# S5's scan by doubling replaced by a turning frame, and the mixer's steps in a new order

## The chip, the cores and the metric

The program runs on one core of a Trainium2 chip. The metric is the device time of one launch in microseconds. The engines are named as the profile names them: PE (TensorE matmul), PEld (its weight load), DVE (VectorE), ACT (ScalarE), POOL (GpSimd), SP (the queue that starts the weight DMAs).

## The reference, cut to what matters

Two transformer blocks run on 256 tokens of width 1024, all in float32. The first block's mixer has four branches (RWKV-7 `a`, spatial gating `b`, short convolution `c`, S5 `d`), whose outputs are gated and summed:

```python
h = rms_norm(x, norm_mix_g) * (1.0 + sc1) + sh1
p = h @ w_in
y_d = s5_mixer(p[..., OFF_D:OFF_G], ...)
gates = sigmoid(p[..., OFF_G:]).reshape(bsz, seq, 4, D_MODEL)
merged = gates[0] * y_a + gates[1] * y_b + gates[2] * y_c + gates[3] * y_d
x = x + gt1 * (merged @ w_o)
```

S5 has 16 groups of 64 complex states, 1024 states in all. Each state follows x[t] = ab * x[t-1] + bu[t] over the 256 tokens:

```python
mag = exp(lam_re * dt)
ab_re, ab_im = mag * cos(lam_im * dt), mag * sin(lam_im * dt)
q = (ab - 1) / lam                      # written out in real and imaginary parts
bb = q[..., None] * b                   # the gain q sits on the input matrix
bu = einsum('gnc,bsgc->bsgn', bb, u)
x = associative_scan(_complex_affine_combine, (ab, bu), axis=1)
y = einsum(c_re, x_re) - einsum(c_im, x_im) + d * u
y_d = glu(gelu(y) @ glu_w)
```

What follows (a feed-forward part, and the second block with its attention and the gathered experts) is not touched.

## The kernel before

The kernel writes one instruction list for each engine by hand. A list runs in order, and engines meet by semaphores. Weights stream through a ring of three slots of 2 MB each, in the order of `STREAM`. The SP queue issues tile n when the tile before it in the same slot has been used.

The mixer's order is the same on all engines. `mixer_order` (L45) walks over 18 projection chunks p0 to p18 (p11 belongs to p10), then over 32 gate parts (8 weight tiles, 2 row tiles, 2 halves), the `ada` sums, the merges, and between them it calls steps. `SCHEDULE` (L30) has one string for each place: `"ad"` behind a chunk means one step of branch a, then one step of branch d. Every engine has a generator for each branch that it serves, and a step is what stands between two `yield`s. So one letter in `SCHEDULE` puts a step at the same place of all lists.

S5's states lie as 8 tiles of 128, worked as four pairs n = 0 to 3. Both kernels have these steps:

- `b_times_u(n)` (PE): the input product into PSUM banks named `bu{n}.0` and `bu{n}.1`.
- `sy{n}` (PE): the output product of pair n. It may start when the scan of the pair is ready. The scan of the next pair may not overwrite its buffers until `sy{n}` is full.
- `add_y(n)` (DVE): adds `sy{n}` to the output.

Before, DVE and ACT scale `bu` by the gain q (L1281, L1902). Then DVE runs eight doubling levels for each pair. A level is four instructions at L1302 and four at L1309 over up to 255 elements, and ACT copies the head that a level leaves as it is (L1914). The powers of `ab` for the levels come from 42 small DVE instructions (L1261 to L1266).

RWKV (branch a) has 42 steps. The first ones are: the shift (DVE L1323, L1326, which tells `shifted`), then PE's transposes of v (`vr`) and three small products that wait for `a6` (ACT L1924, L1925), then the norm of k, the decay (DVE L1338 to L1357) and the bonus (DVE L1362 to L1378, which tells `rk` and `abkr`). Then for each of the two halves of the sequence there are the head products, a transpose `D`, six rounds of one product X and two products Y and Z, which DVE adds at L1400 and L1406, and the outputs. At the end come a layer norm on DVE (L1422 to L1451) and PE's transposes `zA` (L732), which the last merge needs. What is left of branch a when the gate parts are done runs behind them with nothing between.

Matmuls in float32 appear as two records each in the profile, so one gate part of four matmuls is eight records.

## Time and profile before

| | us |
|---|---|
| median of three runs | 1574.41 (1573.51 to 1580.03) |
| the profiled execution, its own time | 1573.48 |
| its span in the trace | 1572.2 |
| first projection starts, last `w_o` product's result added | 40.67, 396.8 |

The mixer, up to the first block's residual sum, takes from 40.67 to about 397 us. Behind it PE waits for the next weight tile (397.2 us), and the rest runs to 1572.2. A span is the time from the first to the last instruction of the trace. A row in brackets such as `[3.64 <-ACT arena L1783]` says how long the engine sat idle ahead of the instruction and which instruction released it. PEclk is the clock that TensorE was granted, as a share of full speed.

### The profile page before, as it was taken

The page shows a single profiled execution, that of the slowest core. Times are in us where ns is not written, and L with a number is a line of the kernel's source. Part 1 is how long each engine was busy: PE and PEld are TensorE (multiplying, and loading weights), DVE is VectorE, ACT ScalarE, POOL GpSimd, SP SyncE. Part 2 cuts the span into 40 slices and gives each one's busy share as a digit, 9 for nine tenths or more (in the row PEclk, how much of TensorE's full clock was granted, in tenths as well). Part 3 has the DMA queues.
Part 4 walks back from the last instruction along what each step waited for, and adds up shares of the span by engine and source line. Part 5 has one row for each costly group of instructions (what it writes and reads, how often), then busy time and mean ns, then how long its engine had stood idle before and what let it go on. Part 6 is the DMA issues. An engine that isn't in the chain of part 4 may idle for free.

```text
span 1572.2 us, 14528 instructions
## 1 busy us (share of the span) xinstructions
PE 1278.0 (81%) x5070; PEld 781.6 (50%) x5070; DVE 908.4 (58%) x1992; ACT 405.3 (26%) x1069; POOL 369.9 (24%) x285
## 2 busy tenths in 40 slices
PE   2989999979999799777787587976897687778775
PEld 2875556644766674476555365434742233233322
DVE  6288877854120211156546569765886777767654
ACT  2152112112100222112212223341333433333322
POOL 0001211210000000023323123231574444454420
PEclk9999999979999898988998688897999999999999
DMA  9633433443788565669999798997999999999995
GB/s 371 237 127 120 164 145 135 186 158 109 295 345 336 181 261 214 241 269 420 416 376 423 277 400 321 358 394 314 398 421 421 421 421 421 421 421 421 421 421 226
DMA packets 56233, 488.51 MB, mean 311 GB/s; under 512 B 6496, under 2 KB 8800, under 8 KB 10080
## 3 DMA queue, kind: packets, MB, share of 16 engines
q0 software_dynamic: 36864, 268.45, 41.6%
q1 hardware_dynamic: 18144, 215.55, 35.5%
q10 hardware_dynamic: 1152, 3.59, 0.6%
q8 instruction: 40, 0.66, 0.2%
q14 instruction: 33, 0.27, 0.0%
HBM read 486.51 MB, written 1.05 MB: 310 GB/s over the span
## 4 chain that ended last, share of the span: by engine, by line
PE 49%; DMA 31%; DVE 13%; issue 3%; ACT 3%; POOL 0%; another core or an unknown queue 0%; ACTq 0%; SPq 0%; DVEq 0%; POOLq 0%
PE ps L448 25%; DMA arena<-in_euv,arena 16%; PE ps L851 7%; DMA ring<-in_w 7%; PE ps L525 6%; PE ps L812 5%; DMA ring<-in_euv,arena 4%; PE ps L978 4%; DVE arena L1039 2%; DVE arena L1302 1%; DVE arena L1689 1%; DMA ring<-in_qkv 1%; DVE arena L1309 1%; DMA ring<-in_wout 1%; DVE xr L1713 1%
## 5 line engine op out<-in xcount | busy, mean ns | idle before, releaser
L2217 POOL DMA_INDIRECT arena<-in_euv,arena x162 | 205.5, 1269 | 650.0 <-DVE arena L1683 335.2
L448 PE MATMUL ps<-arena,ring 128*128 128x128 f32 (+1 forms) x2320 | 319.6, 302 | 26.9 <-DMA ring<-in_w 6.1
L448 PEld LDWEIGHTS ps<-arena,ring 128*128 128x128 f32 x2320 | 306.7, 205 | 47.1 <-issue 10.0
L978 PE MATMUL ps<-arena 128*128 128x512 f32 x424 | 207.1, 632 | 62.8 <-ACT arena L2118 61.9
L1689 DVE CUSTOM_DVE_ANT_0 arena<-arena 128x1024 f32<-128x1024 f32 x162 | 196.5, 1222 | 77.4 <-DMA arena<-in_euv,arena 77.0
L978 PEld LDWEIGHTS ps<-arena 128*128 128x128 f32 x424 | 80.8, 199 | 185.6 <-ACT arena L2118 97.6
L851 PE MATMUL ps<-ring,arena 128*128 128x512 f32 x256 | 123.9, 642 | 32.2 <-DMA ring<-in_w 32.2
L978 PE MATMUL ps<-ring,arena 128*128 128x512 f32 x240 | 116.1, 626 | 29.4 <-ACT arena L2118 29.4
L812 PE MATMUL ps<-ring,arena 128*128 128x512 f32 x256 | 124.0, 636 | 9.6 <-DMA ring<-in_g 3.4
L448 PE MATMUL ps<-arena 128*128 128x128 f32 (+4 forms) x684 | 113.9, 314 | 20.8 <-ACT arena L1783 17.6
L2127 ACT ACTIVATE arena<-arena 128x2 f32<-128x2 f32 x128 | 25.9, 202 | 396.9 <-DVE arena L1689 396.8
L2217 POOL DMA_INDIRECT ring<-in_euv,arena x76 | 95.9, 1262 | 128.7 <-DVE xr L1713 61.5
L448 PEld LDWEIGHTS ps<-arena 128*128 128x128 f32 (+1 forms) x684 | 95.1, 198 | 47.5 <-issue 41.3
L525 PE MATMUL ps<-ring,arena 128*128 128x512 f32 x256 | 116.5, 600 | 0.0
L1689 DVE CUSTOM_DVE_ANT_0 ring<-ring,arena 128x1024 f32<-128x1024 f32 x76 | 92.3, 1223 | 38.4 <-DMA ring<-in_euv,arena 38.1
L448 PE MATMUL ps<-ring,arena 128*128 128x512 f32 (+1 forms) x240 | 103.5, 584 | 7.7 <-DMA ring<-in_bb 2.8
L851 PEld LDWEIGHTS ps<-ring,arena 128*128 128x128 f32 x256 | 51.6, 207 | 95.0 <-issue 61.5
L978 PEld LDWEIGHTS ps<-ring,arena 128*128 128x128 f32 x240 | 46.3, 198 | 96.7 <-issue 51.0
L812 PEld LDWEIGHTS ps<-ring,arena 128*128 128x128 f32 x256 | 51.4, 204 | 69.7 <-issue 57.5
L1713 DVE SCALAR_TENSOR_TENSOR xr<-arena,xr 128x1024 f32<-128x1024 f32 x56 | 71.8, 1283 | 22.1 <-ACT arena L2130 18.7
L1783 ACT COPY arena<-ps 128x512 f32<-128x512 f32 (+1 forms) x71 | 36.0, 509 | 182.0 <-PE ps L448 134.6
L448 PEld LDWEIGHTS ps<-ring,arena 128*128 128x128 f32 x240 | 45.9, 196 | 58.4 <-issue 47.0
(291 smaller groups left out, 1230.6 us busy)
## 6 DMA issues: line engine op xcount, KB each, us to landing
ring<-in_w SPq DMA_DIRECT2D x32, 2048.0 KB, 8.2
ring<-in_ada SPq DMA_DIRECT2D x12, 2048.0 KB, 13.0
ring<-in_qkv SPq DMA_DIRECT2D x12, 2048.0 KB, 7.7
ring<-in_gates SPq DMA_DIRECT2D x8, 2048.0 KB, 7.7
ring<-in_g SPq DMA_DIRECT2D x8, 2048.0 KB, 7.7
ring<-in_pq SPq DMA_DIRECT2D x8, 2048.0 KB, 7.5
ring<-in_wp SPq DMA_DIRECT2D x5, 2048.0 KB, 7.8
ring<-in_wout SPq DMA_DIRECT2D x4, 2048.0 KB, 7.3
```

The lines of the kernel that those rows point to most:

```text
L448: ins = te.matmul(o, l, r, start=(i == 0), stop=(i == len(pairs) - 1))
L525: ins = te.matmul(psum(name)[:], hT[:, k, tt * 128:(tt + 1) * 128], w[:, k * 512:(k + 1) * 512], start=(k == 0), stop=(k == 7))
L812: ins = te.matmul(psum(name)[:], hL[tt][:, k, :], w[:, k * 512:(k + 1) * 512], start=(k == 0), stop=(k == 7))
L851: ins = te.matmul(o[:], fT[:, i % 2, c, :], w[:, c * D + hf * 512:c * D + hf * 512 + 512], start=(i == 0 and c == 0), stop=(i == 7 and c = ...
L978: ins = te.matmul(psum(name)[:], diag[:, added[0] % N_DIAG, :], slots[slot_of[n]][:, D + hf * 512:D + (hf + 1) * 512], start=(fresh[tt] > ...
L1039: ins = v.scalar_tensor_tensor(a, wk, ck, a, ALU.mult, ALU.add)
L1302: first[(i, q)] = done(v.scalar_tensor_tensor(dst[:, i, q, s_:S], src[:, i, q, 0:m], pr_[:, q:q + 1], src[:, i, q, s_:S], ALU.mult, ALU.add))
L1689: ins = v.tensor_tensor_reduce(out=x, in0=x, in1=xn[:, tt, :], scale=1.0, scalar=0.0, op0=ALU.mult, op1=ALU.add, accum_out=hv[:, n % 16:n ...
L1713: added[tt] = slot_done[n] = done(v.scalar_tensor_tensor(xs, slots[slot_of[n]][:, D:2 * D], av[:, n % 32:n % 32 + 1], xs, ALU.mult, ALU.add))
L1783: emptied(sc.copy(dst, psum(name)[:, 0:width]), name)
L2127: done(sc.activation(gl, hv[:, n % 16:n % 16 + GROUP], ACT.Gelu))
L2217: gp.indirect_dma_start(slots[i], None, A["euv"], bass.IndirectOffsetOnAxis(ap=idx[:, n // 16 % 4, e % 16:e % 16 + 1].bitcast(U32), axis=0 ...
```

## The change

The recurrence is rewritten in a frame that turns with each state. With ab = mag * e^(i w), the input at token t is turned back by e^(-i w t), so the rest is a real recurrence with the factor `mag`, one for the real and one for the imaginary part. DVE's scan instruction does that in one piece. The result is turned forward again. The two tables of cos(w t) and sin(w t) (`Vr`, `Vi`, 8 x 128 each) are made by GpSimd with 42 instructions that double the length seven times. They cover 128 tokens, so each pair is scanned in two halves, and six small DVE instructions carry the state from the first into the second, turned by the table's last entry. The gain q now goes onto the output matrix `wC`, on GpSimd too (five instructions for each pair, told as `s5_c`).

A pair is now four steps on DVE: turn back (L1279 x4, L1287, L1288), first half (L1299 x4 and six small), second half (L1299 x4), turn forward (L1319, L1321, L1323, L1324, told as `s5_back`). ACT keeps only the setup and the last gelu.

`SCHEDULE` is a new table, of which two entries show the kind of change:

```
-SCHEDULE = ["", "", "", "", "", "", "", "d", "ad", "d", "ad", "da", ...
+SCHEDULE = ["d", "d", "d", "", "", "", "a", "a", "d", "da", "d", "ad", ...
```

PE, at the first steps of branch a. Before (`arena,ring` rows are projection chunks of eight matmuls, L620 the transposes of v, `arena` rows of 256 the small products and the first `b_times_u`):

```order
L448 MATMUL ps<-arena,ring 128x256 x80
L448 MATMUL ps<-ring,arena 128x256 x16
L620 MATMUL ps<-K,arena 128x128 x4
L448 MATMUL ps<-arena 128x256 x10
L448 MATMUL ps<-arena,ring 128x256 x8
```

And PE at the same place of the changed kernel:

```order
L451 MATMUL ps<-arena,ring 128x256 x64
L623 MATMUL ps<-K,arena 128x128 x4
L451 MATMUL ps<-arena 128x256 x6
L451 MATMUL ps<-arena,ring 128x256 x8
L451 MATMUL ps<-arena 128x256 x4
L451 MATMUL ps<-arena,ring 128x256 x8
L451 MATMUL ps<-arena 128x256 x4
```

The transposes moved from behind p10 to behind p7, which is one chunk behind the chunk that the shift on DVE needs (p6).

PE at the hand-over of pair 2, with waits. Before, at the first hand-over (the row that waits for `s5_level` is `sy0`, behind the head products and ahead of a gate part and the transpose `D`):

```order
L448 MATMUL ps<-arena 128x128 [waits drained4]
L448 MATMUL ps<-arena 128x128 x3
L448 MATMUL ps<-arena 128x256 [waits s5_level,s5_head,l_s5c,drained3]
L448 MATMUL ps<-arena 128x256 x3
L525 MATMUL ps<-ring,arena 128x512 [waits drained0,ring2]
L525 MATMUL ps<-ring,arena 128x512 x3
L661 MATMUL ps<-K,arena 128x128 [waits DT,drained5]
```

Now, at `sy2` (behind the second half of a gate part, then Y and Z of the first round):

```order
L528 MATMUL ps<-ring,arena 128x512 x4
L451 MATMUL ps<-arena 128x128 [waits drained4,drained6]
L451 MATMUL ps<-arena 128x128 x3
L451 MATMUL ps<-arena 128x128 [waits drained5]
L451 MATMUL ps<-arena 128x128 x3
L451 MATMUL ps<-arena 128x256 [waits s5_back,s5_c,drained3]
L451 MATMUL ps<-arena 128x256 x3
L528 MATMUL ps<-ring,arena 128x512 [waits drained0,ring2]
```

And DVE at that place of the changed kernel (L1418 and L1424 add Y and Z, `filled5` is the bank of Z):

```order
L1299 SCALAR_TENSOR_TENSOR arena<-arena,small 128x128 [waits vector]
L1299 SCALAR_TENSOR_TENSOR arena<-arena,small 128x128 x3
L1418 TENSOR_TENSOR arena<-arena,ps 128x512 [waits filled4,drained5,vector]
L1424 TENSOR_TENSOR arena<-arena,ps 128x512 [waits filled5,DT]
L1319 TENSOR_TENSOR arena<-arena 128x1024 [waits vector]
L1321 TENSOR_TENSOR arena<-arena 128x1024 [waits vector]
L1323 TENSOR_TENSOR arena<-arena 128x2x256 [waits vector]
L1324 TENSOR_TENSOR arena<-arena 128x2x256
```

`sy2` stands directly behind Z on PE, and on DVE the turn forward stands behind the adding of Z. The same holds at `sy3`.

PE at the end of branch a. Before (64-column rows are the outputs of the second half, L732 is `zA`):

```order
L471 MATMUL ps<-ones,arena 128x1 x4
L448 MATMUL ps<-arena 128x128 x4
L448 MATMUL ps<-arena 128x64 x24
L732 MATMUL ps<-K,arena 128x128 x4
L448 MATMUL ps<-ring,arena 128x512 x8
```

And now:

```order
L528 MATMUL ps<-ring,arena 128x512 x4
L451 MATMUL ps<-arena 128x64 x12
L528 MATMUL ps<-ring,arena 128x512 x12
L474 MATMUL ps<-ones,arena 128x1 x4
L735 MATMUL ps<-K,arena 128x128 x4
L451 MATMUL ps<-ring,arena 128x512 x8
```

Three gate parts now stand between the last outputs and `zA`.

The diff, cut to its core:

```diff
@@ tensor(): s5 @@
                 for n in range(4):
+                    if n < 3:
+                        b_times_u(n + 1)
+                    yield
+                    yield
+                    yield
                     o = take(f"sy{n}", "s5")
-                    te.wait_ge(sig("s5_level"), 8 * n + 8)
+                    te.wait_ge(sig("s5_c"), 5 * n + 5)
+                    te.wait_ge(sig("s5_back"), n + 1)
...
@@ vector(): s5 @@
+                done(v.tensor_copy(Vr[:, :, 0], s2))
+                tell(v.tensor_copy(Vi[:, :, 0], s4), "s5_turn")
...
+                for n in range(4):
+                    v.wait_ge(sig("s5_table"), 42)
+                    if n:
+                        v.wait_ge(*full(f"sy{n - 1}"))
+                    for q in range(2):
...
+                        for x, table in ((xa, Vr), (xb, Vi)):
+                            ins = v.tensor_tensor(x[:, q, :, :].rearrange("p i (h t) -> p (i h) t", h=2), b4,
+                                                  table[:, 2 * n + q, :].unsqueeze(1).broadcast_to([P, 4, 128]), ALU.mult)
...
+                    done(v.tensor_tensor(xa[:, :, 0, :], xa[:, :, 0, :], xb[:, :, 1, :], ALU.add))
+                    done(v.tensor_tensor(xa[:, :, 1, :], xa[:, :, 1, :], xb[:, :, 0, :], ALU.subtract))
...
+                    yield
+                    for h in range(2):
+                        v.wait_ge(*last_own())
+                        for q in range(2):
+                            for i in range(2):
+                                x = xa[:, q, i, h * 128:(h + 1) * 128]
+                                done(v.tensor_tensor_scan(
+                                    x, mag[:, 2 * n + q:2 * n + q + 1].broadcast_to([P, 128]), x,
+                                    last[2 + i][:, q:q + 1] if h else 0.0, ALU.mult, ALU.add))
...
+                        yield
+                    done(v.tensor_tensor(four[1], four[0], times(Vr, js, 4), ALU.mult))
...
+                    done(v.tensor_tensor(four[0], four[0], times(Vi, js, 4), ALU.mult))
...
+                    tell(v.tensor_tensor(xb[:, :, 1, :], xb[:, :, 1, :], xa[:, :, 0, :], ALU.add), "s5_back")
+                    yield
@@ pool(): s5 @@
+                for lv in range(7):
+                    m = 1 << lv
...
+                    one(s8, i, wi, ALU.mult, "s5_table", made)
+                    one(Vr[:, :, m:2 * m], r, wr, ALU.mult, "s5_table", made)
+                    one(Vr[:, :, m:2 * m], Vr[:, :, m:2 * m], s8, ALU.subtract, "s5_table", made)
+                    one(s8, i, wr, ALU.mult, "s5_table", made)
+                    one(Vi[:, :, m:2 * m], r, wi, ALU.mult, "s5_table", made)
+                    one(Vi[:, :, m:2 * m], Vi[:, :, m:2 * m], s8, ALU.add, "s5_table", made)
@@ sync() @@
-                if n == 9:
+                if n == 7:
                     s5_tile("s5b", 0, wB[0])
...
-                if n in (10, 12):
-                    m = n // 2 - 5
+                if n in (8, 9):
+                    m = n - 8
                     sy.wait_ge(*full(f"bu{m}.1"))
...
-                if n in (13, 17, 21):
-                    m = (n - 13) // 4
+                if n in (10, 12, 13):
+                    m = (10, 12, 13).index(n)
                     sy.wait_ge(*full(f"sy{m}"))
```

## Rows read from the trace of the kernel before

**Rows 1.** The page: the span, and each engine's busy time, share and instructions.
```profile
span 1572.2 us, 14528 instructions
PE 1278.0 (81%) x5070; PEld 781.6 (50%) x5070; DVE 908.4 (58%) x1992; ACT 405.3 (26%) x1069; POOL 369.9 (24%) x285
```

**Rows 2.** Windows of the mixer: stretch, its us, then each engine's busy time, PEclk, DMA.
```profile
100.00:150.00 50.00, 41.61 (x163) 28.95 (x162) 46.20 (x107) 12.79 (x30) 3.10 (x3) 0.93 0.33 116
150.00:260.00 110.00, 106.24 (x423) 62.95 (x423) 85.42 (x187) 18.56 (x45) 22.50 (x14) 1.00 0.42 155
260.00:322.00 62.00, 59.55 (x268) 37.24 (x267) 46.67 (x101) 13.26 (x25) 10.73 (x4) 1.00 0.46 166
322.00:350.00 28.00, 17.74 (x64) 11.31 (x64) 16.75 (x41) 4.49 (x7) 5.07 (x4) 0.70 0.32 109
```

**Rows 3.** PE in order of time: start, length, records, [idle ahead <-who released it].
```profile
113.28 5.41 PE L448 MATMUL ps<-arena,ring 128*128 128x256 f32 x16 [3.64 <-ACT arena L1783]
...
120.26 3.62 PE L448 MATMUL ps<-arena,ring 128*128 128x256 f32 x16
...
138.86 1.02 PE L448 MATMUL ps<-K,arena 128*128 128x2 f32 x8 [2.95 <-DVE arena L1368]
...
150.26 3.60 PE L525 MATMUL ps<-ring,arena 128*128 128x512 f32 x8
...
157.57 1.05 PE L448 MATMUL ps<-arena 128*128 128x128 f32 x8
...
336.40 1.08 PE L732 MATMUL ps<-K,arena 128*128 128x128 f32 x4 [7.93 <-DVE arena L1451]
338.21 9.17 PE L448 MATMUL ps<-ring,arena 128*128 128x512 f32 x16 [0.72 <-issue]
...
348.70 0.70 PE L448 MATMUL ps<-ring,arena 128*128 128x512 f32 x1 [0.53 <-DMA ring<-in_glu]
```

**Rows 4.** SP at the load of the glu weights.
```profile
341.05 0.33 SPq L2268 DMA_DIRECT2D ring<-in_glu  x1
```

**Rows 5.** DVE grouped by line, 40 to 400 us: count, busy us, mean ns, idle.
```profile
L1302 DVE SCALAR_TENSOR_TENSOR arena<-arena 128x255 f32<-128x255 f32 (+7 forms) x128 | 54.4, 487 | 1.3
...
L1139 DVE TENSOR_TENSOR arena<-arena,ps 128x512 f32<-128x512 f32 x12 | 8.1, 686 | 8.8 <-PE ps L448 8.8
```

**Rows 6.** The page's groups: DVE's two-input instruction over 1024 elements.
```profile
L1713 DVE SCALAR_TENSOR_TENSOR xr<-arena,xr 128x1024 f32<-128x1024 f32 x56 | 71.8, 1283 | 22.1 <-ACT arena L2130 18.7
```

**Rows 7.** DVE in order of time: copy of p2, the shift, four scans, one sum.
```profile
53.65 0.42 DVE L1129 COPY arena<-ps 128x256 f32<-128x256 f32 x1 [6.48 <-PE ps L448]
...
68.00 2.03 DVE L1323 TENSOR_TENSOR arena<-arena 128x1792 f32<-128x1792 f32 x1
70.06 2.87 DVE L1326 SCALAR_TENSOR_TENSOR arena<-arena,cols 128x256 f32<-128x256 f32 x7
...
97.11 1.37 DVE L1343 TENSOR_TENSOR_SCAN arena<-ones,arena 128x128 f32<-128x128 f32 x4
...
195.12 1.47 DVE L1042 TENSOR_TENSOR arena<-arena 128x512 f32<-128x512 f32 x1
```

**Rows 8.** Windows over the decay step and over the bonus step.
```profile
96.66:104.70 8.04, 6.24 (x29) 5.19 (x28) 7.80 (x13) 5.26 (x10) 0.00 (x0) 1.00 0.01 2
136.45:141.96 5.51, 3.10 (x12) 1.91 (x13) 5.37 (x11) 0.17 (x1) 0.00 (x0) 0.91 0.00 0
```

**Rows 9.** ACT in order of time: the copy of p7, then from `shifted` to `a6`.
```profile
70.92 0.37 ACT L1783 COPY arena<-ps 128x256 f32<-128x256 f32 x1 [6.48 <-PE ps L448]
...
74.77 1.28 ACT L1924 ACT_TABLE_LOAD   x1
...
77.78 0.41 ACT L1925 ACTIVATE arena<-arena 64x256 f32<-64x256 f32 x1
```

**Rows 10.** POOL in order of time: one instruction alone, one beside a busy DVE.
```profile
150.27 1.09 POOL L2184 TENSOR_TENSOR arena<-arena,K 128x512 f32<-128x512 f32 x1
...
189.93 6.11 POOL L2184 TENSOR_TENSOR arena<-arena,K 128x512 f32<-128x512 f32 x1 [10.18 <-PE ps L448]
```

More of the change, by code:

```diff
@@ L327, in build @@
         W6 = f4(xn)[:, 1024:1792]
+        Vr, Vi = (merged[:, i, :].rearrange("p (a b) -> p a b", a=8) for i in range(2))
+        cs = cs0, f4(xn)[:, 1792:2048].rearrange("p (a b) -> p a b", a=2)
         pb4 = f4(pa)
@@ L1203, in s5 @@
                 lre, lim, dt_, mag, abr, abi, qr, qi = (sp[:, i, :] for i in range(8))
-                s1, s2, s3, s4, s5_, nqi = (sp[:, i, :] for i in range(8, 14))
+                s1, s2, s3, s4 = (sp[:, i, :] for i in range(8, 12))
+                last = [small[:, 98 + 2 * i:100 + 2 * i] for i in range(4)]
                 def one(ins):
@@ L1317, in s5, with last_own @@
                 add_y(3)
                 yield
+                yield
+            def last_own():
+                return own, n_own[0]
             def rwkv():
@@ L1388, in rwkv @@
                         v.wait_ge(*full("St"))
+                    else:
+                        v.wait_ge(sig("vln"), 1)
+                        v.wait_ge(sig("zB"), 1)
+                        v.wait_ge(sig("yc"), 1)
                     masked(f"MT{tt}", MT, su)
@@ L1876, in s5 @@
             def s5():
-                dt_, mag, qr, qi = (sp[:, i, :] for i in (2, 3, 6, 7))
-                s1, s3, s4, s5_ = (sp[:, i, :] for i in (8, 10, 11, 12))
-                yield
+                dt_, mag = sp[:, 2, :], sp[:, 3, :]
+                s1, s2, s3, s4 = (sp[:, i, :] for i in range(8, 12))
                 tell(sc.activation(dt_, cols[:, C_DT:C_DT + 8], ACT.Exp), "s5_dt")
@@ L2195, in pool @@
+            gen_a, gen_d = rwkv(), s5()
             for what, arg in mixer_order():
@@ L2197, in pool @@
                     merge(1)
-                elif what == "step" and arg[0] == "a":
-                    next(gen_a, None)
+                elif what == "p" and arg[0] == CHUNKS[1][0]:
+                    gp.wait_ge(sig("l_K"), 16)
+                    gp.wait_ge(sig("l_ws"), 16)
+                    gp.tensor_tensor(wsT, wsT, bc4(iu), ALU.mult).then_inc(sig("wsT"), 1)
+                elif what == "step" and arg[0] in "ad":
+                    next(gen_a if arg[0] == "a" else gen_d, None)
             for _ in gen_a:
```

197 lines of the change are left out of this document (82 added, 115 removed).

## The prediction

> **What bounds the kernel now.** I read the page first: PE is busy 81% of the span, DVE 58%, and no engine is full [rows 1]. The share says little, because the stages differ, so I read the mixer's windows next [rows 2], then PE in order of time with its waits [rows 3]. From 100 to 322 us PE is busy 207.4 of 222 us. DVE is at 92% from 100 to 150 us and at 75 to 78% after that. So the mixer is bound by PE's own work, and a faster S5 can give back only the time in which PE waits or runs at the low clock. It cannot give back DVE's time: the 128 instructions of L1302 are 54.4 us of DVE, L1309 has as many, but most of them lie beside matmuls [rows 5]. Before the residual sum nothing runs in parallel to the mixer, and what follows starts from it. So I take a microsecond of PE's time here as a microsecond of the whole.
>
> What PE loses now, by stretch:
> - 100 to 150 us: 8.4 us idle, and a granted clock of 0.93, which over 50 us is 3.5 us at full speed. Together 11.9 [rows 2]. The waits seen are for evacuations stuck behind DVE (3.64) and for the bonus (2.95). The first of them was followed by 16 records in 5.41 us, where 16 such records take 3.62 [rows 3]. So a wait of about 3 us or more costs some 1.8 us on top, at the lower of the clock's two levels (1.2 and 2.4 GHz).
> - 150 to 322 us: 3.8 + 2.4 = 6.2 us idle [rows 2].
> - 322 to 350 us: 10.3 us idle [rows 2], of which 7.93 is the layer norm ahead of `zA` [rows 3]. The clock of 0.70 falls partly on idle time. The merge behind it took 9.17 us for 16 records that need 6.9 (twice the 3.60 for 8, less the pipeline's end of one) [rows 3], so 2.3 lost there, and by my estimate 1.5 in the small products just before.
>
> **What the change takes away.** All of the 11.9, since DVE and ACT no longer hold evacuations behind levels. The 6.2 too (they are single waits for levels, merges and evacuations). At the end three gate parts (24 records, 10.3 us at 3.44 each) now run beside the layer norm, so the 7.9 goes, with about 1.1 of small gaps and the 3.8 of low clock: 12.8. What is late next is the glu weight. It was issued at 341.05 [rows 4] and PE waited 0.53 for it at 348.70 [rows 3]. Its slot is freed by an `ada` sum on DVE that follows the layer norm, and this chain is not shortened. The last output product ended at about 328.4 in this trace. Counted from there PE reaches glu after 10.3 + 0.9 + 1.1 + 6.9 + 0.9 = 20.1 us and the weight lands after about 21.6. That gives 1.3 back against before. Sum of what goes: 11.9 + 6.2 + 12.8 - 1.3 = **29.6 us**.
>
> **What the change adds.** It moves hand-overs to places where PE has nothing else in its list. I walked PE and DVE from wait to wait with these durations.
> - *Start of branch a.* The shift begins with p6 at 68.0 and ends at 72.9 [rows 7]. p7 ends at 70.9 [rows 9]. The transposes (0.45) now stand behind p7, and `a6` behind them comes 3.4 us after `shifted` (from 74.77 to 78.19, two table loads) [rows 9], at 76.3. Before, three more chunks covered this. PE waits 76.3 - 70.9 - 0.45 = 5.0, then 0.5 more for the evacuation of p8, which `b_times_u(0)` needs, and pays 1.8 at the low clock: 7.3.
> - *sy0.* From the first bank of `bu0` PE has 21.5 us of work up to p13 (each chunk 3.44). DVE has: turn back 4.0 (four from PSUM at 0.69 as L1139 [rows 5], two more, overlapping by 0.08), the decay step 8.04 [rows 8], first half 2.2 (four scans 1.37 [rows 7] and six small), the bonus step 5.5 [rows 8], second half 1.4, gating's statistics 1.4, turn forward 3.9. The last is two products over 1024 elements and two sums of 0.69. For the 1024 the nearest row is 1.28 [rows 6], which I take; by the rate of the shift's first instruction (2.03 for 1792 elements) it would be 1.16 [rows 7]. Sum 26.4, so PE waits 5.0 and pays 1.8: 6.8.
> - *sy1.* From the start of sy0 PE has 18.9 us. DVE must wait for gating's two banks at 12.0, and then has 0.9 + 0.75 + 2.2 + 1.4 + 3.9 behind them: 21.4. PE waits 2.6. Half of the time the clock falls: 0.9. Together 3.5.
> - *sy2 and sy3.* Both stand directly behind product Z on PE, while DVE's list has the turn forward behind the adding of Z. So however long DVE has been free, PE waits for 0.2 + 0.6 (adding) + 3.9 + 0.1 = 4.8, and 1.8 of clock: 6.6 each, 13.2. This is the surest term.
> - *Transpose D of the second half* now has X directly behind it: 0.85 for the evacuation.
>
> These are 7.3 + 6.8 + 3.5 + 13.2 + 0.85 = 31.7 us.
> - *The tables.* GpSimd starts when `s5_turn` is told, behind the copy of p2 at 53.65 [rows 7] and some 0.7 us of small instructions, at 54.8. It makes 42 dependent instructions over 8 to 512 elements, 6,096 elements in all. The trace shows only 512 elements, at 1.09 us [rows 10]. Purely by size the 42 take 13.0 us; at 1.09 each they take 45.8. Six of them are of that size, 24 are of 64 elements or fewer. I take 30, nearer to the middle since the fixed part must be something: ready at 84.8. DVE needs them when `bu0` is full, at about 85.7. But the shift (4.9 us) and the norm of k run just before, and a GpSimd instruction beside a busy DVE took 6.11 instead of 1.09 [rows 10]. That puts the tables at about 87.5, so 1.8 us late, and all of it reaches sy0. Above: 45.8 + 6 gives 106, 20 late. Below: nothing.
> - *DVE beside GpSimd.* The sum that met this GpSimd instruction took 1.47 instead of 0.69 [rows 7]. I count 0.8 for each of two such meetings in the chain to sy0 and one in the shift: 2.4, and between 0 and 4.
> - *The queue SP.* The two S5 tiles now stand ahead of wp4, which waits until `bu0` is full (about 87) and lands near 95. p16 needs it at about 119. gates 4, behind the next tile, waits for p10 anyway. Covered by 20 us; nothing counted. POOL's five products for `wC` (3.6 us each pair by size) have over 15 us at each pair.
>
> The trace shows that GpSimd was held up exactly while DVE ran instructions with two inputs in SBUF. By the Trainium skill, SBUF — State Buffer, "SBUF: two separate sides", DVE and GpSimd share one pair of ports, held for a whole instruction by whoever starts first. The rows agree. By that rule the tables and the shift would delay one another instruction by instruction, up to 0.5 us for each of the shift's eight, 4 us where I count 0.8, and the sum would be 3.2 higher.
>
> [...]
>
> **Sum.** 31.7 + 1.8 + 2.4 = 35.9 added, 29.6 taken away: +6.3. I take off 0.8 because the clock's loss can't fall fully on all of five waits (8.1 us counted): +5.5. The profiled execution took 1573.5, 0.9 below the median of 1574.4. Forecast: **1579.0**.
>
> **The rivals.**
> - *The tables come late.* GpSimd's small instructions cost nearly as much as its large ones. For it: 42 instructions in one chain, each with a semaphore, and a busy DVE beside them. Against it: most are tiny. It decides from about 0.74 us an instruction (31 us in all); at 1.0 the tables are ready at 97 + 2, 13 us behind `bu0`, instead of 1.8: 1590. DVE is held at the first turn back, and the decay, the bonus and sy0 behind it. This is the side of slower.
> - *Clean hand-overs.* The clock stays up through the new waits (7.3 saved), the tables are in time and GpSimd is in nobody's way (1.8 + 2.4 saved), and DVE's chains to sy0 and sy1 are each 1 us shorter than rows of other operands say: 1579 - 13.5 = 1565.5. For it: the waits of 2 us and less in this trace were followed by a clock of 1.00 [rows 2]. Against it: all but one of the new waits are near 5.
> - *Nothing moves.* Gains and new waits cancel because a stretch of PE that I count as waiting is covered: the clock stays up at two waits (3.6) and the tables are ready in time (1.8): 1573.5. For it: both are within the working above.
>
> **How the numbers follow.** Chances: the forecast (waits traded for waits) 0.47, with its own range 1574 to 1587; late tables 0.17; clean hand-overs 0.14; nothing moves 0.22. About 0.5% is what a measurement of this kernel tells from no change: 1566.5 and 1582.3. Faster is the clean hand-overs and little else: 0.13. Slower is the late tables and somewhat under half of the forecast's upper side: 0.17 + 0.18 = 0.35. The same: 0.52. The range goes from the clean case to the late tables: 1564 to 1591.
>
> **What would show it.** PE idle of about 5 us ahead of the first products that need `a6`, of 5 ahead of sy0, 2 to 3 ahead of sy1, and 4.8 ahead of sy2 and sy3, each released by DVE's last instruction of the turn forward, with PEclk below 1 behind them. The 7.93 ahead of `zA` gone, and a wait for glu of 1 to 2 us. GpSimd's table done at 85 to 90 us, and the first turn back right behind it. DVE's busy time in the mixer down by about 75 us with no such gain in the span. I am wrong if `sy2` shows no wait (then DVE is ahead of PE in a way that its list forbids), if the front loses more than 20 us, or if something behind the mixer moves by itself.

## The result, and the profile after

The changed kernel takes 1583.72 us (median of 19 runs, 1573.21 to 1590.08), the kernel before 1573.51 (19 runs, 1567.70 to 1580.31). The ratio is 1.0061, with an interval of 1.0044 to 1.0078: slower by about 10 us. The forecast was 1579.0 in a range of 1564 to 1591. The profiled execution is the fastest of the 19, 1573.21 us. That matters below: read alone, its span of 1571.9 us (1572.2 before) would say that nothing happened.

The same four windows as [rows 2], of the changed kernel (stretch, its us, then busy time of PE, PEld, DVE, ACT and POOL with counts, PEclk, DMA share, GB/s):

```profile
100.00:150.00 50.00, 42.07 (x178) 35.42 (x177) 38.75 (x84) 10.02 (x19) 4.46 (x5) 0.90 0.29 99
150.00:260.00 110.00, 100.66 (x417) 62.17 (x416) 56.55 (x97) 13.69 (x22) 20.71 (x22) 0.95 0.34 125
260.00:322.00 62.00, 61.27 (x258) 36.66 (x257) 15.11 (x23) 7.48 (x13) 10.29 (x9) 1.00 0.45 170
322.00:350.00 28.00, 26.73 (x98) 14.86 (x97) 18.61 (x46) 5.79 (x9) 0.69 (x1) 0.94 0.66 236
```

DVE is busy 66 us less in these windows (195.0 before, 129.0 after). Part of that only moved to earlier places: over the first 400 us it is 57.8 less (265.9 before, 208.1 after). PE idles 9.3 us from 150 to 260, where it idled 3.8, and nearly as much as before in front of that (7.9, where it was 8.4). The end is better: 0.7 us idle instead of 2.4 from 260 to 322, and 1.3 instead of 10.3 behind that.

PE in order of time, at the waits that the prediction names (start, length, records, idle ahead and who ended it):

```profile
77.82 1.08 PE L623 MATMUL ps<-K,arena 128*128 128x128 f32 x4 [6.83 <-DVE arena L1339]
79.90 4.27 PE L451 MATMUL ps<-arena 128*128 128x256 f32 x12 [0.99 <-ACT arena L1911]
...
88.28 1.97 PE L451 MATMUL ps<-arena 128*128 128x256 f32 x8 [0.66 <-ACT arena L1798]
...
116.22 3.75 PE L451 MATMUL ps<-arena 128*128 128x256 f32 x8 [5.22 <-DVE arena L1324]
...
140.19 3.15 PE L451 MATMUL ps<-arena 128*128 128x256 f32 x8 [2.71 <-DVE arena L1324]
...
174.12 3.75 PE L451 MATMUL ps<-arena 128*128 128x256 f32 x8 [4.67 <-DVE arena L1324]
...
201.94 3.45 PE L451 MATMUL ps<-arena 128*128 128x256 f32 x8 [4.67 <-DVE arena L1324]
...
342.74 0.63 PE L735 MATMUL ps<-K,arena 128*128 128x128 f32 x4
344.65 8.80 PE L451 MATMUL ps<-ring,arena 128*128 128x512 f32 x16 [1.27 <-issue]
...
355.44 12.26 PE L451 MATMUL ps<-ring,arena 128*128 128x512 f32 x24 [1.21 <-DMA ring<-in_glu]
```

Eight records of an `sy` product take 1.97 us at the full clock (the row at 88.28 has the same shape, and a granted clock of 1.00). They take 3.45 to 3.75 behind a wait of about 5, 3.15 behind 2.71 and 1.97 behind 0.66. The granted clock over the four `sy` rows is 0.50, 0.60, 0.50 and 0.55. The wait of 7.93 ahead of `zA` [rows 3] is gone, but 24 glu records take 12.26 us. In the kernel before:

```profile
348.70 10.57 PE L448 MATMUL ps<-ring,arena 128*128 128x512 f32 x24 [0.53 <-DMA ring<-in_glu]
```

GpSimd and DVE of the changed kernel around the table, in order of time:

```profile
54.84 23.78 POOL L2191 TENSOR_TENSOR arena<-arena 128x8 f32<-128x8 f32 x42 [54.39 <-DVE arena L1247]
78.59 1.31 POOL L2231 TENSOR_TENSOR arena<-arena,K 128x512 f32<-128x512 f32 x1
```
```profile
68.11 2.04 DVE L1336 TENSOR_TENSOR arena<-arena 128x1792 f32<-128x1792 f32 x1
70.18 7.50 DVE L1339 SCALAR_TENSOR_TENSOR arena<-arena,cols 128x256 f32<-128x256 f32 x7
77.78 2.26 DVE L1346 TENSOR_SCALAR arena<-arena,cols 128x256 f32<-128x256 f32 x2
...
89.49 0.69 DVE L1279 TENSOR_TENSOR arena<-ps,arena 128x512 f32<-128x512 f32 x1 [8.44 <-PE ps L451]
```

The table is ready at 78.6. DVE's first turn back starts 11 us later, and what it waited for is PE's `bu0`. The table is not late, but it has a price: beside it the seven instructions of the shift take 7.50 us, where they took 2.87 [rows 7].

**One number for the mixer.** The first record of L854 (L851 before) follows directly on the mixer. Its start, the *mark*, moves only with what lies ahead of it. Before, after, and the changed kernel profiled once more:

```profile
L851 PEld LDWEIGHTS ps<-ring,arena x256: 186/190/338, 415.0 to 874.7; 128*128 128x128 f32 x128
```
```profile
L854 PEld LDWEIGHTS ps<-ring,arena x256: 186/190/338, 422.6 to 879.1; 128*128 128x128 f32 x128
```
```profile
L854 PEld LDWEIGHTS ps<-ring,arena x256: 186/190/338, 426.1 to 885.4; 128*128 128x128 f32 x128
```

All kernels, in us. "At glu" is when PE had nothing left but glu (the start of its 24 records less the wait ahead of them). "Behind" is the span less the mark. The ratio compares all runs with those of the kernel before on the same chip.

```
kernel             at glu  glu wait  mark    span    behind   median   ratio [interval]
before             348.2   0.5       415.0   1572.2  1157.2   1573.5
changed            354.2   1.2       422.6   1571.9  1149.3   1583.7   1.0061 [1.0044, 1.0078]
e0_again           354.4   3.2       426.1   1582.0  1155.9   1585.4   1.0076 [1.0052, 1.0100]
e1_swap            351.5   3.1       421.9   1578.0  1156.1   1578.9   1.0036 [1.0016, 1.0055]
e2_late_a          350.2   3.1       421.8   1579.6  1157.8   1578.8   1.0019 [0.9998, 1.0039]
e4_old_tail        363.6   0.8       430.0   1585.2  1155.2   1586.9   1.0094 [1.0070, 1.0119]
e6_early_table     354.3   1.6       421.5   1575.1  1153.6   1584.4   1.0080 [1.0052, 1.0108]
e7_order           346.2   2.0       415.5   1571.9  1156.4   1572.8   1.0012 [0.9989, 1.0035]
e8_both            341.9   1.4       410.4   1567.7  1157.3   1569.4   0.9987 [0.9967, 1.0006]
e9_tail            340.6   3.9       412.9   1566.4  1153.5   1571.9   0.9994 [0.9977, 1.0012]
e10_pool_behind    351.4   3.0       423.1   1578.2  1155.1   1575.5   1.0036 [1.0017, 1.0054]
e11_best           330.4   3.0       400.5   1552.0  1151.5   1554.0   0.9903 [0.9875, 0.9932]
e12_glu_first      329.6   0         397.6   1553.0  1155.4   1557.0   0.9895 [0.9867, 0.9922]
```

What lies behind the mark takes 1151 to 1158 us in every kernel but for the first profile of the changed one, 1149.3. So that execution was quick in the part that the change doesn't touch, and the loss at the mark (7.6 and 11.1 us in the two profiles, against the one profile of before) is of the size of the loss of 10 in the medians. In both profiles about 6 us of it are there already at glu.

### The profile page after: what moved, and what is told of

The parts are those of the page before. It is cut to its first block, busy times and chain, and to the rows that moved or that the text cites. A ratio compares the mean times of both kernels' runs of the same rounds, so it can differ in the third digit from the quotient of the medians.

```text
span 1571.9 us, 14270 instructions
## 1 busy us (share of the span) xinstructions
PE 1279.0 (81%) x5070; PEld 783.5 (50%) x5070; DVE 852.9 (54%) x1772; ACT 388.8 (25%) x1019; POOL 395.2 (25%) x347
## 3 DMA queue, kind: packets, MB, share of 16 engines
HBM read 486.51 MB, written 1.05 MB: 310 GB/s over the span
## 4 chain that ended last, share of the span: by engine, by line
PE 45%; DMA 31%; DVE 7%; issue 3%; POOL 2%; ACT 2%; another core or an unknown queue 0%; SPq 0%; DVEq 0%; ACTq 0%
PE ps L451 22%; DMA arena<-in_euv,arena 18%; PE ps L528 7%; PE ps L854 7%; DMA ring<-in_w 7%; PE ps L815 5%; PE ps L981 2%; DMA ring<-in_euv,arena 2%; POOL arena L2251 1%; DVE arena L1707 1%; DMA ring<-in_qkv 1%; DVE xr L1731 1%; DMA ring<-in_wout 1%; POOL ring L2251 1%; DMA ring<-in_bb 1%
## 5 line engine op out<-in xcount | busy, mean ns | idle before, releaser
L451 PE MATMUL ps<-arena,ring 128*128 128x128 f32 (+1 forms) x2320 | 317.2, 300 | 22.2 <-DMA ring<-in_qkv 6.5
L451 PEld LDWEIGHTS ps<-arena,ring 128*128 128x128 f32 x2320 | 304.5, 204 | 41.5 <-issue 9.1
L451 PE MATMUL ps<-arena 128*128 128x128 f32 (+4 forms) x684 | 120.2, 324 | 34.3 <-DVE arena L1324 17.3
L854 PE MATMUL ps<-ring,arena 128*128 128x512 f32 x256 | 124.1, 643 | 29.5 <-DMA ring<-in_w 29.5
L451 PEld LDWEIGHTS ps<-arena 128*128 128x128 f32 (+1 forms) x684 | 98.9, 202 | 63.9 <-issue 57.5
L451 PE MATMUL ps<-ring,arena 128*128 128x512 f32 (+1 forms) x240 | 104.3, 589 | 8.0 <-DMA ring<-in_bb 3.0
L854 PEld LDWEIGHTS ps<-ring,arena 128*128 128x128 f32 x256 | 51.7, 207 | 92.4 <-issue 61.5
L1798 ACT COPY arena<-ps 128x512 f32<-128x512 f32 (+1 forms) x71 | 35.9, 510 | 229.3 <-PE ps L451 185.8
L1731 DVE SCALAR_TENSOR_TENSOR xr<-arena,xr 128x1024 f32<-128x1024 f32 x56 | 71.8, 1282 | 21.4 <-ACT arena L2116 18.0
L451 PEld LDWEIGHTS ps<-ring,arena 128*128 128x128 f32 x240 | 46.5, 197 | 59.2 <-issue 49.3
```

The lines of the kernel that those rows point to most:

```text
L451: ins = te.matmul(o, l, r, start=(i == 0), stop=(i == len(pairs) - 1))
L854: ins = te.matmul(o[:], fT[:, i % 2, c, :], w[:, c * D + hf * 512:c * D + hf * 512 + 512], start=(i == 0 and c == 0), stop=(i == 7 and c = ...
L1731: added[tt] = slot_done[n] = done(v.scalar_tensor_tensor(xs, slots[slot_of[n]][:, D:2 * D], av[:, n % 32:n % 32 + 1], xs, ALU.mult, ALU.add))
L1798: emptied(sc.copy(dst, psum(name)[:, 0:width]), name)
```

## The experiments

Where an edit adds a line (e6 and e8 to e12), line numbers behind it are one higher: L1340 is L1339, L452 is L451. Behind a second added line they are two higher.

**e0_again.** No edit.

> The changed kernel once more, nothing edited. In its first profile the first record of the late products (L854) starts at 422.8 us, 7.7 later than before (415.1), yet that execution's span equals the one of before (1571.9 and 1572.2), while its 19 times have a median 10 us above before. Theory A (the new waits in the mixer are the cost, and the weight stream behind it varies from run to run): the mark stays at 422.8 within 1 us, whatever the total; a total of 1580 or more lies behind 423 us, mostly in waits for transfers. Rival B (the loss varies inside the mixer, by how GpSimd's and DVE's instructions meet): in an execution near 1583 the mark is at 430 or later.

Median 1585.4. The mark was 426.1, so theory A's "within 1 us" failed, and so did B's 430. Up to the tail the trace is the old one (waits of 6.84, 0.98, 0.67, then 17.3 over four at the `sy` products; PE is at glu within 0.2 us). The 3.5 us come from glu:

```profile
357.66 13.42 PE L451 MATMUL ps<-ring,arena 128*128 128x512 f32 x24 [3.24 <-DMA ring<-in_glu]
```

The wait is 2.0 longer and the records behind it 1.2. Issued at 348.58, the weight took 9.1 us to land, against 7.6 in the first profile. Of the 10.1 us between the two spans, 6.6 lie behind the mark. They are not mostly waits for transfers, as theory A had it: from 430 us on, 46.9 us of PE's waits end with a transfer in the first profile and 49.1 in the second.

**e1_swap.** At the entries behind the fourth and last part of gates 4 and of gates 5:

```diff
-            "cca", "ad", "ad", "ad", "ad", "ad", "ad", "ad", ...
+            "cca", "ad", "ad", "da", "ad", "ad", "ad", "da", ...
```

> At the two places where a product step of branch a and a step of S5 stand behind one gate part (sy2 and sy3), S5's step now comes first. Theory A: DVE's turn forward then runs beside the gate part, PE's waits of 4.67 and 4.67 us ahead of sy2 and sy3 go to under 0.7, the low clock behind them too (2 x 1.8), and one wait of up to 1.5 us for the product behind the turn forward comes in their place: the mark (first L854) moves from 422.8 to 411 to 414, the total by -9 to -12 us against the changed kernel. Rival B (DVE has no free time before those places, or what stood behind now waits instead): the wait moves to products Y and Z, mark at 419 or later, total within 3 us. Rival C (behind the mixer the weight stream sets the pace and takes up every shift): mark earlier by 9 or more, total the same within 3 us.

```profile
169.91 3.75 PE L451 MATMUL ps<-arena 128*128 128x256 f32 x24 [1.61 <-DVE arena L1324]
...
196.51 6.41 PE L451 MATMUL ps<-arena 128*128 128x256 f32 x24 [4.58 <-DVE arena L1324]
```

`sy2` went as theory A has it (4.67 to 1.61), `sy3` as rival B has it. Between the two, DVE's list in order of time:

```profile
174.37 0.88 DVE L1039 TENSOR_SCALAR arena<-ring,cact 128x512 f32<-128x512 f32 x2
175.16 5.56 DVE L1042 SCALAR_TENSOR_TENSOR arena<-ring,cact,arena 128x512 f32<-128x512 f32 x6
180.76 1.10 DVE L1045 TENSOR_TENSOR arena<-arena 128x512 f32<-128x512 f32 x1
181.78 2.47 DVE L1279 TENSOR_TENSOR arena<-ps,arena 128x512 f32<-128x512 f32 x4
...
195.67 0.69 DVE L1324 TENSOR_TENSOR arena<-arena 128x512 f32<-128x512 f32 x1
```

It has no idle time here: `ada` sum 4 (7.5 us) stands ahead of the turn back of pair 3. At `sy3` the prediction's reason, "directly behind product Z", was one of two causes. With it removed the other, DVE's own chain, holds PE as long. PE is at glu 2.9 us before e0_again. The mark of 421.9 is rival B's; the median, 6.6 lower, lies between the two.

**e2_late_a.** Branch a's first products behind p9 and p10.

```diff
-SCHEDULE = ["d", "d", "d", "", "", "", "a", "a", "d", "da", "d", "ad", ...
+SCHEDULE = ["d", "d", "d", "", "", "", "", "", "d", "ad", "aad", "ad", ...
```

> The first three steps of branch a stand behind projections 9, 10, 10 instead of 6, 7, 9; the first S5 product stays behind p8. Theory A: PE runs p8 and p9 while DVE shifts, so the 6.83 + 0.99 us of waiting at 78 to 80 us go to under 1 and the low clock with them; bu0 is full 8 us earlier, DVE's idle 8.4 us before its first turn back goes, and the wait of 5.2 ahead of sy0 stays at 3 to 6 since both engines move together: mark at 413 to 416, total -6 to -10 us against the changed kernel. Rival B (DVE's chain, held up by the shift of 7.5 and 2.26 us beside GpSimd's table, is the bound, and PE only waits elsewhere): the wait ahead of sy0 grows by about 7, mark at 421 or later, total within 2 us.

```profile
105.04 1.84 PE L451 MATMUL ps<-K,arena 128*128 128x2 f32 x8 [8.08 <-DVE arena L1381]
...
115.11 1.96 PE L451 MATMUL ps<-arena 128*128 128x256 f32 x8 [2.99 <-DVE arena L1324]
```

The waits at 78 us are gone and one of 8.08 ahead of the bonus product has come. DVE's decay step waits 6.84 us for ScalarE, whose input is made by the products that now stand behind p10. It starts at 92.4, only 1.1 us earlier than without the edit (93.4), so what PE gained at 78 us it loses at the bonus. The mark moved by 4.3 against e0_again, between the two theories. The start of the branch is a loop through PE, ScalarE and DVE, and moving one end of it moves the wait.

**e4_old_tail.** Three entries near the end, so that three steps of branch a run behind the gate parts:

```diff
-            ..., "a", "a", "a", "a", "a", "a", "a", "a"]
+            ..., "a", "", "", "", "a", "a", "a", "a"]
```

> The last three steps of branch a in front of the layer norm stand three gate parts later, so that nothing of PE's lies beside the layer norm, as in the kernel before. Theory A (the prediction's term of 12.8 - 1.3 for the tail is right): the wait of about 7.9 ahead of zA comes back, with the low clock behind it, and the wait of 1.2 for the glu weight goes: mark at 432 to 436 (+10 to +12), total +8 to +12 us. Rival B (the tail was worth less, since the idle time only moved to the glu and merge products behind): mark later by under 6 us.

```profile
340.92 2.79 PE L451 MATMUL ps<-arena 128*128 128x64 f32 x24
...
352.08 1.09 PE L735 MATMUL ps<-K,arena 128*128 128x128 f32 x4 [7.54 <-DVE arena L1469]
...
364.45 10.57 PE L451 MATMUL ps<-ring,arena 128*128 128x512 f32 x24 [0.82 <-DMA ring<-in_glu]
```

The wait came back, and PE is at glu 9.2 us later than in e0_again. Yet the mark moved by only 3.9, since the wait for glu is 2.4 shorter and its records run at the full clock, 2.9 shorter: rival B. (Against the first profile the mark moved by 7.4; the median is 1.5 above that of e0_again.) From the last outputs (340.92 here, 324.16 before, 328.95 and 329.65 in the two profiles of the changed kernel) to the end of glu's 24 records, less the 10.3 us of gate parts that the changed kernel has between them, it is 34.1 here, 35.1 before, 28.5 and 31.1 in the changed kernel. So the new tail is worth 6.6 or 4.0 us, where the prediction had 11.5.

Why glu comes late shows on DVE and ScalarE, in the changed kernel and then in e4_old_tail:

```profile
337.48 0.20 DVE L1448 RECIPROCAL small<-small 128x8 f32<-128x8 f32 x1 [3.23 <-ACT small L1959]
```
```profile
335.33 0.60 ACT L1881 ACTIVATE arena<-ps 128x512 f32<-128x512 f32 x1 [3.17 <-PE ps L528]
```
```profile
346.94 0.20 DVE L1448 RECIPROCAL small<-small 128x8 f32<-128x8 f32 x1 [0.27 <-ACT small L1959]
```

With the gate parts beside the layer norm, ScalarE takes the bank of the first of them (L1881) ahead of the layer norm's square root (L1959). DVE waits 3.23 us for the root in all nine profiles with this tail, and 0.27 in e4_old_tail and in the kernel before. The `ada` sum behind the layer norm, which frees glu's slot, is later by as much: glu is issued 16.1 us behind the last output in the changed kernel (at 347.88), 13.0 in e4_old_tail and 12.6 before.

**e6_early_table and e10_pool_behind.** S5's setup ahead of p0, and then also GpSimd's next work behind the shift:

```diff
     steps = iter(SCHEDULE)
+    yield from (("step", ("d",)) for _ in range(3))
```
```diff
                 elif what == "p" and arg[0] == CHUNKS[1][0]:
+                    gp.wait_ge(sig("shifted"), 1)
                     gp.wait_ge(sig("l_K"), 16)
```

> S5's three small setup steps stand in front of projection 0 instead of behind projections 0, 1 and 2, nothing else moves. GpSimd can then start its table at about 48 us instead of 55. Theory A (the shift took 7.50 us instead of 2.87 only because GpSimd ran its last, large table instructions at the same time): the table is ready by 69, the seven instructions of L1339 take 2.9, the two of L1346 0.6, PE's wait of 6.8 ahead of the transposes (L623) falls to about 2.2, and everything behind it comes 4 to 5 us earlier: mark (first L854) at 416 to 422 where the unchanged kernel had 422.6 and 426.1, total -3 to -5 us against it. Rival B (the scalar-by-tensor form is slow for its new place or operands, not for GpSimd): L1339 stays at 7.5 and the wait at 6.8; total the same.

> As the kernel with the early table, and GpSimd waits for the shift (the semaphore shifted) before its mask product for wsT and its first five products for wC, which stood beside the shift there (L2232 3.04 us, L2192 4.44 us for 5). GpSimd then does nothing from 69.5 us until the shift is over. Theory A (two-input instructions of DVE and GpSimd's instructions hold one another up, whatever GpSimd computes): L1337 takes 2.03 (2.91 with the early table), the seven of L1340 take 2.9 (6.17), PE's wait ahead of the transposes falls from 6.4 to 2.2, and its wait for a6 behind them grows to 3 since ScalarE's two table loads come next; mark 1 to 3 us earlier than with the early table (421.5), at 419 to 421. Rival B (the shift is slow in its new place for another reason): L1340 stays above 5.

GpSimd and DVE of e6_early_table, then of e10_pool_behind:

```profile
47.76 21.72 POOL L2192 TENSOR_TENSOR arena<-arena 128x8 f32<-128x8 f32 x42 [47.31 <-DVE arena L1248]
69.44 3.04 POOL L2232 TENSOR_TENSOR arena<-arena,K 128x512 f32<-128x512 f32 x1
72.44 4.44 POOL L2192 TENSOR_TENSOR arena<-arena 128x256 f32<-128x256 f32 x5
...
71.40 6.17 DVE L1340 SCALAR_TENSOR_TENSOR arena<-arena,cols 128x256 f32<-128x256 f32 x7
```
```profile
47.64 21.73 POOL L2192 TENSOR_TENSOR arena<-arena 128x8 f32<-128x8 f32 x42 [47.19 <-DVE arena L1248]
74.23 1.27 POOL L2233 TENSOR_TENSOR arena<-arena,K 128x512 f32<-128x512 f32 x1 [4.86 <-DVE arena L1340]
...
71.28 2.86 DVE L1340 SCALAR_TENSOR_TENSOR arena<-arena,cols 128x256 f32<-128x256 f32 x7
```

With the table out of the way the shift still took 6.17, since GpSimd went straight on to its next products, and its mask product in turn took 3.04 instead of 1.27. With GpSimd idle it took 2.86. This isolates the cause: it is GpSimd at work beside DVE, whatever GpSimd computes. Part of the loss only moves: the two DVE instructions behind the shift then took 2.00 and 1.05 us beside GpSimd's products, where they took 0.62 and 0.69 in e6. PE's wait fell from 6.37 to 2.76, and the one for `a6` stayed at 0.99, where 3 was expected. Of the two marks, that of e10 is 3.0 before that of e0, with glu alike, but 1.6 behind that of e6, where 1 to 3 us ahead was expected. The difference is glu: e6 had a wait of 1.6 and the full clock behind it, e10 3.0 and 13.60 us for the 24 records. At glu e10 is 2.9 ahead of e6, and e6 0.1 ahead of e0. So the early table alone gives nothing (1.0080 in the total), and with GpSimd made to wait it gives 3 us at glu (1.0036; the medians of the two differ by 9.0, more than the profiles show).

**e7_order and e8_both.** Order alone, then order with the early table (of e7 the first two lines of the list, then of e8):

```diff
+SCHEDULE = ["d", "d", "d", "", "", "", "", "", "d", "aad", "a", "d", "abd", "b", "b", "d", "d", "d",
+            "dcca", "da", "ad", "ad", "ad", "a", "da", "ad", "ad", "ad", "da", "ad", "ad", "ad", "a", "a", "aa",
```
```diff
+SCHEDULE = ["", "", "", "", "", "", "", "a", "dada", "", "d", "ad", "b", "b", "bd", "d", "d", "d",
+            "dcca", "ad", "ad", "ad", "a", "da", "ad", "ad", "ad", "da", "ad", "ad", "ad", "a", "a", "a", "aa",
```

> Only the order of steps: branch a's first products behind p9, the four sy steps 1 to 3 chunks or parts later and ahead of the product of branch a that stands at the same place. Theory A (the mixer's new waits come from too little distance between what DVE needs and where PE asks; DVE itself has room): all five waits of 5 us go to under 1.5 each, DVE is the limit only up to 110 us; mark at 402 to 409, total -14 to -20 us against the unchanged kernel, so 1567 to 1572. Rival B (DVE is the bound through the whole S5, ada sum 4 included, as sy3 in the swap experiment: DVE had no idle time from 173.8 to 196.4 us there): waits of 3 or more stay at sy2 or sy3 or move to Y and Z; mark 413 or later, total -10 at the most. Rival C (the weight stream sets the pace behind the mixer, so earlier ends are not passed on): mark 402 to 409 but total above 1574.

> The early table and an order built on it: the shift ends at 73, a6 at 75, branch a's first two products and both first S5 products stand behind p8, sy0 behind p15, sy1 behind the first part of gates 4, sy2 and sy3 behind parts of gates 5 and 2. Theory A: the mixer ends as in the order-only kernel or up to 3 us earlier, mark at 400 to 407, total 1562 to 1570, that is 4 to 12 us faster than the kernel before. Theory B (DVE-bound): no better than 1574, since DVE has as much to do. If GpSimd's table in DVE's free time saves DVE some 6 us in the front, DVE's idle time between 70 and 110 us shows it.

Order alone wins back what the change lost (1.0012, mark 415.5), less than theory A expected: waits of 2.2 to 3.2 stay at all four `sy` products, and one of 4.0 is new ahead of the bonus product. These are rival B's numbers; e11 tests its reason. In e8 `sy1` does not wait any more, but there are waits ahead of `bu0`, `sy0` and `sy2`, and the mark of 410.4 lies behind the 400 to 407 of theory A:

```profile
80.08 3.75 PE L452 MATMUL ps<-arena 128*128 128x256 f32 x8 [5.22 <-ACT arena L1799]
...
122.07 3.39 PE L452 MATMUL ps<-arena 128*128 128x256 f32 x8 [5.69 <-DVE arena L1325]
...
174.07 6.43 PE L452 MATMUL ps<-arena 128*128 128x256 f32 x24 [4.88 <-DVE arena L1325]
```

ScalarE's copy of p8 stood behind its wait for the shift (6.17 us again). DVE waited 4.05 and 3.53 us for gating's inputs with the turn forward ready behind them. So ahead of `sy0` DVE's list order was the bound, not its work.

**e9_tail.** Of e8: branch a one part earlier at the end, `ada` sums 7 and 8 ahead of `mod` 6 and 7 on DVE.

```diff
                 elif what == "mod":
+                    if arg[0] > 5:
+                        ada_sum(arg[0] + 1)
...
```

> As the one with both, and in the tail branch a one gate part earlier, and DVE's ada sums 7 and 8 in front of the two small sums over PE's products that they do not need. Theory A (glu's weight is late because its slot is freed by ada sum 8, which waits for a product at the end of gates 1): glu is issued 5 us earlier (348.6 in the unchanged kernel against zA at 343.4), the wait of 3.2 for it goes, with up to 1.8 us at the low clock: mark 3 to 5 us earlier than with both alone, total as much. Rival (the tile of ada 9, which now shares the queues, or the residual sum behind becomes late): less than 1.5 us.

```profile
330.71 0.33 SPq L2305 DMA_DIRECT2D ring<-in_ada  x1
331.08 0.43 SPq L2305 DMA_DIRECT2D ring<-in_glu  x1
...
344.49 13.36 PE L452 MATMUL ps<-ring,arena 128*128 128x512 f32 x24 [3.92 <-DMA ring<-in_glu]
```

The second line is issued 4.5 us earlier than in e8 and lands 1.2 later; what differs is that the two tiles are now issued 0.4 us apart instead of 5.8. DVE's wait for the layer norm's root is 0.27 here too, and PE is at glu 1.3 us before e8, but the mark is 2.5 later. The rival holds: no gain (0.9994; e8 0.9987).

**e11_best.** E8's order with `sy0` ahead of gating's second step, `sy2` and `sy3` a part later, and e10's wait:

```diff
+SCHEDULE = ["", "", "", "", "", "", "", "a", "dada", "", "d", "ad", "b", "", "db", "d", "bd", "d",
+            "dcca", "ad", "ad", "ad", "a", "a", "da", "ad", "ad", "ad", "da", "ad", "ad", "ad", "a", "a", "aa",
```

> The early table, GpSimd behind the shift, and S5's steps spread once more: sy0 behind p15 and in front of gating's second step, on which DVE waited 4.05 + 3.53 us for ScalarE and PE in the kernel with both; sy2 and sy3 one part later. Theory A (the mixer's waits are a matter of distance alone): waits ahead of bu0 (5.2 there), sy1 (5.7) and sy2 (4.9) fall to under 1.5 each, and with them 3 to 5 us of low clock; mark at 395 to 401 (410.4 there), total 1552 to 1560, about 1% faster than the kernel before. Theory B (DVE-bound from 100 to 180 us): mark 405 to 410 and total within 4 us of the kernel with both, 1569. Rival C (from mark on the stream of weights sets the end, so that less than half of a gain in the mixer arrives): mark under 402 and total above 1563.

PE waits that are left (total, times, longest, in us):

```profile
PE ps L452 <- DVE arena L1325: 6.9, 3, 3.0
...
PE ps L452 <- DMA ring<-in_glu: 3.0, 1, 3.0
...
PE ps L452 <- ACT arena L1799: 1.7, 1, 1.7
```

The four `sy` waits were 17.3 in the changed kernel and are 6.9 over three. `sy0` is the one without a wait; its 5.69 in e8 is what the expectation calls the wait of `sy1`. Of the three waits that theory A named, `sy0` and `sy2` (1.2) are under 1.5 and `bu0` is at 1.7, but `sy1` has 2.7 and `sy3` 3.0. The mark is 400.5, the median 1554.0, the ratio 0.9903 [0.9875, 0.9932]. It beats both kernels, by 1.0% and 1.6% (the second from the two ratios). Theory B (DVE the bound through S5) and rival C fall: the mark is 14.5 us ahead of the kernel before and the median 15.8. No run has the old scan in the new order, so how much of the 15.8 us the turning frame gives, and how much the order alone would give to the old scan, stays open.

**e12_glu_first.** Of e11, glu's tile one place earlier in the stream:

```diff
-    names += [("ada", 8), ("o_ab", 1), ("ada", 9), ("glu", 0), ...
+    names += [("ada", 8), ("o_ab", 1), ("glu", 0), ("ada", 9), ...
```

> The best kernel so far (1554.0 median), with one edit in the order of the weight stream: glu's tile is fetched before the tile of ada 9, not behind it. It takes the slot that the end of gates 1 frees (318.8 us there) instead of the one that ada sum 8 frees (324.6), and w_o 1 now waits for glu's slot instead of ada 9's. Theory A (glu's lateness, and with it part of the tail's missing gain, is only that its slot comes free behind DVE's ada sum 8): glu lands 5 to 6 us earlier, PE's wait of 3.0 for it goes, and the 1.7 us at the low clock behind it: mark 4 to 5 us earlier (396 where it was 400.5), total 1549 to 1551. Rival (the transfers behind one another are the limit, as with the tail experiment, where glu was issued 4.5 us earlier together with ada 9 and landed no earlier): the wait goes but comes back ahead of w_o 1 or the small sum over ada 9; mark within 1.5 us, total the same.

```profile
329.64 10.78 PE L452 MATMUL ps<-ring,arena 128*128 128x512 f32 x24
342.23 1.09 PE L468 MATMUL ps<-K,arena 128*128 128x128 f32 x8 [1.80 <-DVE arena L1511]
```

No wait ahead of glu and no low clock behind it; 1.8 us come back at the next transposes. The mark is 2.9 earlier, between theory A's 4 to 5 and the rival's 1.5. In the total this can't be told from e11 (0.9895 against 0.9903, intervals that overlap almost wholly).

## Why the prediction was right, and where it was not

The forecast's mechanism held: waits were traded for waits, the four at `sy` released by the turn forward. It put the median 4.7 us too low: 5.5 us more than the kernel before, where 10.2 were measured. That it came so near is in part luck, since errors in single terms cancel.

- **sy0, sy1, sy2, sy3** (6.8, 3.5, 6.6, 6.6): measured 5.22, 2.71, 4.67 and 4.67 of waiting and 1.8, 1.2, 1.8 and 1.5 at the low clock, so 7.0, 3.9, 6.5 and 6.2. (The terms given for `sy1` add up to 21.15 and not 21.4, which changes it by 0.25.) E1 qualifies the reason at `sy3`.
- **Start of branch a** (7.3): 8.5 of waiting and 2.0 at the low clock, 10.5. Most of the wait (6.83) stands ahead of the transposes, which need the shift, and 0.99 ahead of the products that need `a6`, where the walk had all 5.0.
- **DVE beside GpSimd** (2.4, of it 0.8 in the shift): the shift alone lost 4.6. This is why the start of branch a came out high: e10 takes PE's wait from 6.4 to 2.8. By the Trainium skill, SBUF — State Buffer, "SBUF: two separate sides", the engines share ports held for a whole instruction, from which the prediction had 4 us as the other value. The runs agree with that, and the 0.8 from a single meeting [rows 7] was too little.
- **The tables** (+1.8, ready at 87.5): not late, ready at 78.6. I took 30 us for the 42 instructions; moved ahead of the shift they took 21.7. The 1.8 is nothing, and the late-tables rival did not occur. The first turn back was not "right behind" the table either, but 11 us later, behind `bu0`.
- **D/X** (0.85): 0.72.
- **Sum of what is added** (35.9): 34.8. Right, with errors that cancel: the start of branch a 3.2 too low, the tables and DVE beside GpSimd 4.2 too high, since what GpSimd cost stands in the waits.
- **The tail** (12.8 less 1.3, 11.5): 6.6 in the first profile, 4.0 in the second, and this is the term that was mis-sized. The prediction said of the chain to glu's slot that it "is not shortened". It became longer: e4_old_tail shows DVE's wait of 3.23 us for ScalarE, which is 0.27 without the gate parts. So glu's records began 23.7 and 25.2 us behind the last output, where the walk had 21.6. They then took 12.26 and 13.42 us instead of 10.57 (granted clock 0.86 and 0.79), which the walk did not have.
- **The tail's sum** (11.5) was also 1.0 above its own walk: glu 1.3 later with 10.3 us of gate parts in between is 9.0, and 1.5 for the small products (measured 1.51) makes 10.5. That is 1.0 + 2.1 + 1.7 = 4.8 and 1.0 + 3.6 + 2.9 = 7.5, and 4.9 and 7.5 are missing. The forecast's error of 4.7 is of this size.
- **The merge and the wait for glu.** The merge behind `zA` ran at 0.81 of the clock in the first profile (8.80 us) and at 1.00 in the second (3.67 and 3.70, with 0.92 between), but PE was at glu at the same time within 0.2 us. The wait for glu (1.5 by the walk) was 1.2 to 2.0 in four profiles with this tail and 3.0 to 3.2 in five; why the weight takes 7.6 us to land in one and 9.1 in another stays open.
- **Taken away in the front and middle** (11.9 + 6.2 = 18.1): with mark, sum and tail as measured, 20.6 and 19.7 (34.8 - 7.6 - 6.6 and 34.8 - 11.1 - 4.0). This is a remainder, but the windows bear it out: from 100 to 322 us PE's idle time after (7.93, 9.34, 0.73) is the new waits and nothing else (5.22 + 2.71, 4.67 + 4.67, 0.72), so all the idle time of before is gone.
- **DVE's busy time in the mixer** (down by about 75): down by 57.8 over the first 400 us.
- **Clean hand-overs** did not occur as built, but the experiments came near: with the steps spread by a few places, the table earlier and GpSimd held back beside the shift, the same work gives 1554, with 6.9 us of waits left at `sy`.

That the whole follows the mixer was assumed; the table's column "behind" shows it, over marks from 397.6 to 430.0. Why that part varies by 6 to 8 us from one execution to the next was not tried and stays open.

## What to carry to other kernels

Taking work off a busy engine pays only where its results are asked for no sooner than they can be there. Here a kernel with 58 us less of DVE work in the mixer was 10 us slower in one order of the steps and 16 us faster in another (with the table made earlier and GpSimd held back beside the shift), so count the distance between producer and consumer in microseconds of the consumer's own work at each hand-over, with everything that stands ahead in the producer's list. Idle time given back is worth less than its length where the next weight is late and the clock is low behind its wait. Work put beside a chain can lengthen the chain on a third engine: look at every engine that the chain passes. One profile can lie far from the median; find a mark behind the changed part and compare there.

## What the runs showed of the hardware

- GpSimd's 42 dependent instructions over 8 to 512 elements took 21.7 us with the shift beside only the last 1 us of them, 0.52 each, and 23.8 with the shift beside the last 10 us.
- Seven DVE instructions over 256 elements with two inputs in SBUF: 2.86 us with GpSimd idle, 6.17 beside its products, 7.50 beside the table.
- Two DVE instructions with one tensor input in SBUF (L1346) took 2.26 us beside the end of the table and the product behind it, and 0.62 with GpSimd idle (e6).
- Eight records that take 1.97 us at the full clock took 3.45 to 3.75 behind waits of 4.7 to 5.2, 3.15 behind 2.71, and 1.97 behind 0.66.
- Of two weight tiles issued 0.4 us apart the second landed after 13.4 us; glu's tile, issued 5.8 us behind the other in e8, took 7.8.
